# Two narrow projection slots: tokens stationary, or weights stationary and turned back

## The chip, the cores and the metric

The kernel runs on one core of a Trainium2 chip. The metric is the device time of one execution in microseconds (us). Five engines work side by side: TensorE (PE; its weight loads are listed apart as PEld), VectorE (DVE), ScalarE (ACT), GpSimd (POOL), and SyncE (SP), whose queue issues the DMAs here. Engines are ordered only by semaphores that the kernel sets and waits for by hand.

## The reference, cut to what matters

The network has 512 tokens of 1024 channels and eight sublayers: an even mixer, a SwiGLU, an odd mixer, a SwiGLU, an SSM mixer (Mamba-2), a SwiGLU, a convolution module and a SwiGLU. Each begins with a norm. Two places of it are touched.

In the even mixer one projection makes nine things from the normed tokens `h`:

```
aq, ak, av, bq, bk, bv, iq, ik, iw = split(h @ w_in, (512, 512, 512, 512, 64, 64, 512, 64, 8))
score = sum_h relu(iq_h @ ik.T * 64**-0.5) * (iw_h * 8**-0.5)      # picks the top 128 keys
yb    = softmax(bq_h @ bk.T ... over the picked keys) @ bv
```

`bv` (64 columns, the values) and `iw` (8 columns, the weights of the index heads) are needed with tokens on the partitions. In the SSM mixer the projection has 5152 columns, of which the last 32 are the time steps:

```
z, xbc, dt = split(h @ w_in, (2048, 3072, 32))
dt = softplus(dt + dt_bias)                 # (512 tokens, 32 heads)
a  = -exp(a_log);  y = scan(xs * dt, dt * a, bm, cm)
```

`dt`, too, is needed with tokens on the partitions. Everything is float32.

## The kernel before

**Layout.** `x_cm`, `h_hi` and `h_lo` hold activations channel-major: 8 chunks of 128 channels on the partitions, 512 tokens along the free axis. A normed activation is kept as two parts, `h_hi` (rounded to the float32r format) and `h_lo` (the rest).

**Slots.** Weights stream through two buffers in slots of up to 8 chunks of rows by 256 columns. For slot n SP loads `w_raw` (`load_slot`, L552 to L558; it waits until slot n-2 is split), ACT rounds it to `w_hi` in two halves (`round_half`, L1746 to L1758; it waits until slot n-2 is used), POOL subtracts to get `w_lo` in two halves (`low_part`, L804 to L810), and PE multiplies. `widths` names the two slots that are narrower than 256 columns: slot 1 with 72 and the first SSM slot with 32. ACT and POOL work on that width only. A product is three float32r matmuls per chunk: hi by hi, hi by lo, lo by hi.

**Two ways to multiply a slot.** `slot_cm` and `half_cm` keep 128 weight columns stationary and stream 512 tokens: 24 matmuls for 128 columns, and the result is channel-major. `slot_tok` (L1180 to L1194) keeps 128 tokens stationary and streams the weight columns: for each of 4 token tiles, 8 chunks, three matmuls, so 96 matmuls whatever the width, and the result is token-major, as `bv`, `iw` and `dt` want it.

```
for i in range(NT):
    for k in range(SLOT_K):
        pe.matmul(dst[i], h_hi[:, k, P*i:P*i+P], w_hi[parity][:, k, 0:width], ...)
        pe.matmul(dst[i], h_lo[:, k, P*i:P*i+P], w_hi[parity][:, k, 0:width], ...)
        pe.matmul(dst[i], h_hi[:, k, P*i:P*i+P], w_lo[parity][:, k, 0:width], ...)
```

**Even mixer.** `project` on PE (from L1272) runs slots 0 to 11 in order; slot 0 makes `bk` and `ik`, slot 1 `bv` and `iw`, slots 2 and 3 `iq`, slots 4 to 9 `bq`, `aq`, `ak`, slots 10 and 11 `av`. After each slot `after_even` sums one group of the conditioning projection (`ada_sums`, L1238), and after slot 2 `later_rows` turns parameter rows and waits for a scalar from DVE. ACT copies results out (`even_dest`, L1962), rounds the slot after next, and takes the roots for the head norms. DVE does the reciprocals of the head norms, a conditioning group of eight steps per slot (`ada_group`), and from slot 4 on adds index scores and takes the top keys (`index_add`, `take_top`).

**SSM mixer.** `ssm_pe` (L834) multiplies the dt slot first, each of its first 8 chunks as the norm on DVE delivers it (`h_chunk`, semaphore `h_ready`), into banks 0 and 1. Then come pieces d = 0 to 5 of a prologue (24 matmuls of 512 columns each, into bank d mod 3), with three small matmuls for the decays after d = 1 (L957), and then a scan of 18 steps in which further pieces fill gaps. DVE adds the bias to dt (L2070) when all 96 matmuls are done, and with ACT makes softplus and the log decay (L2073 to L2077). Piece 0 waits until DVE has read bank 0, and ACT rounds the slot of pieces 2 and 3 when the dt slot is used.

The order of work on every engine is fixed by the text of the program; no planner moves it.

Of the kernel before, what the change touches and what calls it, by code (L numbers as in the profile page):

```python
# [18 lines left out]
ALU = mybir.AluOpType  # L19
ACT = mybir.ActivationFunctionType  # L20
# [16 lines left out]
DI = 2048  # L37
MH = 32
# [87 lines left out]
def build(nc, t, out, sublayers=8):  # L126

    with ExitStack() as ctx:
        def sem(name):
            return ctx.enter_context(nc.semaphore(name))  # L130
# [206 lines left out]
        y_root = sem("y_root")  # L337
        sink_step = sem("sink_step")
        dt_step = sem("dt_step")
        dt_act = sem("dt_act")  # L340
        decay_sums = sem("decay_sums")
        decay_ready = sem("decay_ready")
# [149 lines left out]
        def ssm_loads(sp, load_slot):  # L492
            w = t["ssm_w_in_2"][0]
            n = SLOT["ssm"]
            load_slot(n, [(0, w[:, DI + 3072:DI + 3072 + MH])])
            for g in range(MG):
                at = n + 1 + 5 * g
                for j in range(2):
                    c0 = DI + S * g + SLOT_W * j
                    load_slot(at + j, [(0, w[:, c0:c0 + SLOT_W])])  # L500
                c0 = 2 * DI + P * g
                load_slot(at + 2, [(0, w[:, c0:c0 + P]), (P, w[:, c0 + S:c0 + S + P])])
                for j in range(2):
                    c0 = S * g + SLOT_W * j
                    load_slot(at + 3 + j, [(0, w[:, c0:c0 + SLOT_W])])
            for j, (m, k) in enumerate(OUT_ORDER):
                load_slot(SLOT["ssm_out"] + j, [(0, t["ssm_w_out_2"][0][1024 * k:1024 * k + 1024, 256 * m:256 * m + 256])])
# [3 lines left out]
        def _(sp):  # L511
# [60 lines left out]
            def load_swiglu(f):  # L572
# [31 lines left out]
                with sp.Fori(0, 2) as i:  # L604
# [8 lines left out]

            we = t["w_in_even"][0]
            even = [[(0, we[:, BK:BK + HD]), (64, we[:, BK:BK + HD]), (128, we[:, IK:IK + HD]), (192, we[:, IK:IK + HD])],
                    [(0, we[:, BV:BV + HD]), (64, we[:, IW:IW + I_HEADS])]]
            for c0 in (IQ, BQ, AQ, AK, AV):
                even += [[(0, we[:, c0 + 256 * j:c0 + 256 * j + 256])] for j in range(2)]
            for g in range(3):
# [50 lines left out]
        for g_ in range(MG):  # L670
            tok_slots |= {SLOT["ssm"] + 1 + 5 * g_ + 3, SLOT["ssm"] + 1 + 5 * g_ + 4}
            parts_of[SLOT["ssm"] + 1 + 5 * g_ + 2] = 2
        widths = {1: 72, SLOT["ssm"]: MH}
        loads_upto = {}
        count = [0, 0]
        for n in range(SLOT["end"]):
# [154 lines left out]
                        low_part(i * 6 + (n + j), (n + j) % 2, 8 if j % 3 < 2 else FC - 16, SLOT_W)  # L831
                n += N_DOWN

        def ssm_pe(pe, take, freed, slot_tok, slot_cm, h_chunk, follows):  # L834
            n0 = SLOT["ssm"]

            for m in range(2):
                take(m, dt_step, 1)
            dst = [bank[i // 2][:, SLOT_W * (i % 2):SLOT_W * (i % 2) + MH] for i in range(NT)]
            slot_tok(n0, dst, MH, h_chunk(4))  # L840

            def turn(d):

# [106 lines left out]
            for d in range(PROLOGUE):  # L950
                for f in range(8):
                    piece(d, f)
                if d == 1:
                    pe.wait_ge(dt_step, 3)
                    take(5, decay_ready, 1)
                    for j, tri in enumerate((upto, after, ones)):
                        ins = pe.matmul(bank[5][:, P * j:P * j + P], tri[:], log_decay[:].rearrange("p i h -> p (i h)"),  # L957
                                        start=True, stop=True)
                    ins.then_inc(decay_sums, 1)
# [176 lines left out]
        def _(pe):  # L1136
# [33 lines left out]
            def half_cm(n, m, dst):  # L1170
# [6 lines left out]
                    ins = pe.matmul(dst[:], lo, h_hi[:, k, :], start=False, stop=k == SLOT_K - 1)  # L1177
                ins.then_inc(w_used, 1)

            def slot_tok(n, dst, width, before=None):  # L1180

                parity = n % 2
                pe.wait_ge(w_split, 2 * n + 2)
                for i in range(NT):
                    for k in range(SLOT_K):
                        if before is not None and i == 0:
                            before(k)
                        a_hi_, a_lo_ = h_hi[:, k, P * i:P * i + P], h_lo[:, k, P * i:P * i + P]
                        b_hi_, b_lo_ = w_hi[parity][:, k, 0:width], w_lo[parity][:, k, 0:width]
                        pe.matmul(dst[i], a_hi_, b_hi_, start=k == 0, stop=False)  # L1190
                        pe.matmul(dst[i], a_lo_, b_hi_, start=False, stop=False)
                        ins = pe.matmul(dst[i], a_hi_, b_lo_, start=False, stop=k == SLOT_K - 1)
                    if i % 2 == 1:
                        ins.then_inc(w_used, 1)  # L1194
# [77 lines left out]
            def project(parts, nh, base_slot, qk_sq0, qk_root0, qk0, plain0, after_slot=None):  # L1272
# [12 lines left out]
                for s, part in enumerate(parts):  # L1285
                    n = base_slot + s
                    banks = (chunk % 4, (chunk + 1) % 4)
                    before = h_chunk(nh) if s == 0 else None
                    if part[0] == "tok":
                        width = part[1]  # L1290
                        per = 1 if width > P else 0
                        for m in range(2):
                            take(banks[m], plain_copied, plain0 + plain + 1 + m)
                        dst = [bank[banks[i // 2]][:, SLOT_W * (i % 2):SLOT_W * (i % 2) + width] for i in range(NT)]
                        slot_tok(n, dst, width, before)
                        plain += 2
                        while pending:
                            head_sums()
                    else:
                        dst = []  # L1300
                        for m in range(2):
                            if part[m] == "qk":
                                dst.append(take(banks[m], qk_normed, qk0 + qk + 1 + (m if part[0] == "qk" else 0)))
                            else:
                                plain += 1
                                dst.append(take(banks[m], plain_copied, plain0 + plain))
                        if before is not None:
                            slot_cm(n, n % 2, lambda k: h_hi[:, k, :], lambda k: h_lo[:, k, :], dst, before=before)
                        for m in range(2):
                            if before is None:  # L1310
                                half_cm(n, m, dst[m])
                            while pending:
                                head_sums()
                            if part[m] == "qk":
                                pending.append((qk_sq0 + qk, qk_root0 + qk))
                                qk += 1
                    chunk += 2
                    if after_slot is not None:
                        after_slot(s)
# [163 lines left out]
            def after_even(s):  # L1483
# [3 lines left out]
                if 4 <= s < 10:  # L1487
                    pe.wait_ge(plain_copied, 7)
                    for v in range(4 * (s - 4), 4 * (s - 4) + 4):
                        index_scores(v)  # L1490

            EVEN_PARTS = [("qk", "plain"), ("tok", 72), ("plain", "plain"), ("plain", "plain"), ("qk", "qk"), ("qk", "qk"),
                          ("qk", "qk"), ("qk", "qk"), ("qk", "qk"), ("qk", "qk"), ("tok", 256), ("tok", 256)]
            project(EVEN_PARTS, 0, 0, SQ_BASE["even"], ROOT_BASE["even"], 0, 0, after_even)

# [31 lines left out]
            if n_sub > 3:  # L1527
                swiglu(1, 3, follows(4))
            if n_sub > 4:
                ssm_pe(pe, take, freed, slot_tok, slot_cm, h_chunk, follows)  # L1530
            if n_sub > 5:
                swiglu(2, 5, follows(6))
            if n_sub > 6:
# [11 lines left out]
        def ssm_act(act, round_half):  # L1545
            n0 = SLOT["ssm"]
            act.wait_ge(bcast_in, 16 * 8)
            act.activation(alog_row[:], alog_row[:], ACT.Exp).then_inc(dt_act, 1)
            for m in range(2):
                round_half(n0 + 2, m)  # L1550

# [178 lines left out]
        def _(act):  # L1730
# [78 lines left out]
            def project(parts, base_slot, sq0, root0, qk0, dests, after_slot=None):  # L1809
# [12 lines left out]

                for s, part in enumerate(parts):
                    n = base_slot + s
                    if part[0] == "tok":
                        for m in range(2):
                            act.wait_ge(w_used, 2 * n + m + 1)
                            dests(s, m)
# [133 lines left out]
            def even_dest(s, m):  # L1962
                if s == 0:
                    act.activation(ik[:], bank[1][:], ACT.Copy).then_inc(plain_copied, 1)
                elif s == 1:
                    v = bank[2 + m][:].rearrange("p (i w) -> p i w", i=2)
                    act.activation(bv[:, 2 * m:2 * m + 2, :], v[:, :, 0:HD], ACT.Copy)
                    act.activation(iw[:, 2 * m:2 * m + 2, :], v[:, :, HD:HD + I_HEADS], ACT.Copy,
                                   scale=I_HEADS ** -0.5).then_inc(plain_copied, 1)
                elif s in (2, 3):  # L1970
                    c = 2 * (s - 2) + m
                    act.activation(iq[:, c, :], bank[(2 * s + m) % 4][:], ACT.Copy).then_inc(plain_copied, 1)
                else:
# [18 lines left out]
                    act.activation(neg_logit[v % 2][:, 0:w], bank[5 + v % 2][:, 0:w], ACT.Relu, scale=HD ** -0.5  # L1992
                                   ).then_inc(idx_relu, 1)

            EVEN = [("qk", "plain"), ("tok",), ("plain", "plain"), ("plain", "plain")] + [("qk", "qk")] * 6 + [("tok",), ("tok",)]
            project(EVEN, 0, SQ_BASE["even"], ROOT_BASE["even"], 0, even_dest, index_relu)
            act.wait_ge(w_used, 2 * N_EVEN)
            attention(2, 1, dict(s=0, t=0, y=0), A_HEADS, 0, lambda i: P * (i + 1), "diff", back=2)
# [64 lines left out]
        def ssm_dve(dve, link):  # L2063
            n0 = SLOT["ssm"]
            bc_tile = lambda row: row.unsqueeze(1).to_broadcast([P, NT, MH])

            dve.wait_ge(w_used, 2 * n0 + 2)
            for m in range(2):
                v = bank[m][:].rearrange("p (i w) -> p i w", i=2)[:, :, 0:MH]
                ins = dve.tensor_tensor(dt_tok[:, 2 * m:2 * m + 2, :], v, dtb_row[:].unsqueeze(1).to_broadcast([P, 2, MH]), ALU.add)  # L2070
            ins.then_inc(dt_step, 1)
            dve.wait_ge(dt_step, 1)
            dve.scalar_tensor_tensor(out=dt_abs[:], in0=dt_tok[:], scalar=-1.0, in1=dt_tok[:], op0=ALU.mult, op1=ALU.max  # L2073
                                     ).then_inc(dt_step, 1)
# [702 lines left out]
```

## Time and profile before

| | us |
|---|---|
| three runs | 3062.31, 3065.33, 3065.77 |
| median | 3065.33 |
| span of the profiled execution | 3062.3 |
| PE busy | 2800.6 (91% of the span) |
| DVE busy | 1417.1 (46%) |
| ACT busy | 1071.9 (35%) |
| POOL busy | 1077.0 (35%) |

The span runs from the first to the last instruction of the profiled execution; nothing else of that execution's own time is given beside it. The clock column of the profile is the share of full speed that was granted to TensorE: 1.00 is 2.4 GHz and 0.50 is 1.2 GHz. Start times of successive matmuls tell what each one costs in a dense stream, because their listed durations overlap.

### The profile page before, as it was taken

The page shows a single profiled execution, that of the slowest core. Times are in us where ns is not written, and L with a number is a line of the kernel's source. Part 1 is how long each engine was busy: PE and PEld are TensorE (multiplying, and loading weights), DVE is VectorE, ACT ScalarE, POOL GpSimd, SP SyncE. Part 2 cuts the span into 40 slices and gives each one's busy share as a digit, 9 for nine tenths or more (in the row PEclk, how much of TensorE's full clock was granted, in tenths as well). Part 3 has the DMA queues.
Part 4 walks back from the last instruction along what each step waited for, and adds up shares of the span by engine and source line. Part 5 has one row for each costly group of instructions (what it writes and reads, how often), then busy time and mean ns, then how long its engine had stood idle before and what let it go on. Part 6 is the DMA issues. An engine that isn't in the chain of part 4 may idle for free.

```text
span 3062.3 us, 34663 instructions
## 1 busy us (share of the span) xinstructions
PE 2800.6 (91%) x12655; PEld 2262.4 (74%) x12655; DVE 1417.1 (46%) x2167; ACT 1071.9 (35%) x1745; POOL 1077.0 (35%) x535
## 2 busy tenths in 40 slices
PE   4985689999999988999999999999999999799998
PEld 3764357777787667888878888888888765588886
DVE  6489872455412784222123566523331279533312
ACT  2221432322323474333223555523332322433321
POOL 1321000344443223444423565544444321144442
PEclk6897656999999999999988999999999999899998
DMA  7431040355433101223221221123322221122231
GB/s 215 138 110 55 1 138 14 97 164 164 137 100 85 63 28 56 83 82 110 94 74 55 69 69 56 56 83 100 105 91 92 86 63 41 42 96 96 96 97 55
DMA packets 277694, 264.50 MB, mean 86 GB/s; under 512 B 23020, under 2 KB 276557, under 8 KB 277581
## 3 DMA queue, kind: packets, MB, share of 16 engines
q1 hardware_dynamic: 277581, 262.97, 27.0%
q8 instruction: 74, 1.21, 0.2%
q14 instruction: 39, 0.32, 0.0%
HBM read 260.85 MB, written 2.10 MB: 86 GB/s over the span
## 4 chain that ended last, share of the span: by engine, by line
PE 71%; DVE 14%; issue 7%; DMA 3%; ACT 2%; POOL 2%; SPq 1%; DVEq 0%; ACTq 0%; POOLq 0%
PE bank L1151 17%; PE bank L1153 16%; PE bank L1152 16%; DMA root<-in_ada_w_dram 2%; DVE ada_acc L2392 2%; POOL w_lo L809 2%; PE bank L1099 1%; PE bank L883 1%; PE bank L885 1%; PE bank L884 1%; DVE bank L2216 1%; PE bank L1509 1%; DVE root L2398 1%; PE bank L1440 1%; DVE score L2575 1%
## 5 line engine op out<-in xcount | busy, mean ns | idle before, releaser
L809 POOL TENSOR_TENSOR w_lo<-w_raw,w_hi 128x1024 fp32r<-128x1024 f32 (+1 forms) x364 | 865.6, 2387 | 1674.2 <-ACT w_hi L1758 1103.3
L1151 PE MATMUL bank<-h_hi,w_hi 128*128 128x512 f32 x1632 | 651.6, 399 | 25.8 <-DVE h_lo L2359 11.6
L1152 PE MATMUL bank<-h_lo,w_hi 128*128 128x512 f32 x1632 | 645.4, 395 | 0.0
L1153 PE MATMUL bank<-h_hi,w_lo 128*128 128x512 f32 x1632 | 644.6, 395 | 0.0
L1758 ACT ACTIVATE w_hi<-w_raw 128x1024 fp32r<-128x1024 f32 (+1 forms) x232 | 232.2, 1014 | 510.7 <-PE bank L1153 438.9
L1151 PEld LDWEIGHTS bank<-h_hi,w_hi 128*128 128x128 f32 x1632 | 312.7, 192 | 95.7 <-issue 25.0
L1152 PEld LDWEIGHTS bank<-h_lo,w_hi 128*128 128x128 f32 x1632 | 313.1, 192 | 66.3 <-issue 1.7
L1153 PEld LDWEIGHTS bank<-h_hi,w_lo 128*128 128x128 f32 x1632 | 312.3, 191 | 66.5
L1153 PE MATMUL bank<-a_hi,w_lo 128*128 128x512 f32 x704 | 274.2, 389 | 0.0
L1151 PE MATMUL bank<-a_hi,w_hi 128*128 128x512 f32 x704 | 274.2, 389 | 0.0
L1152 PE MATMUL bank<-a_lo,w_hi 128*128 128x512 f32 x704 | 274.2, 389 | 0.0
L1927 ACT ACTIVATE w_hi<-w_raw 128x1024 fp32r<-128x1024 f32 x176 | 182.8, 1052 | 158.4 <-PE bank L1153 157.2
L2454 DVE TENSOR_TENSOR tmp<-sq,bank 128x512 f32<-128x512 f32 x88 | 60.5, 688 | 381.9 <-PE bank L1153 375.9
L2458 DVE TENSOR_TENSOR a_lo<-tmp,a_hi 128x512 f32 x88 | 167.4, 1914 | 22.0 <-ACT a_hi L1942 21.4
L1152 PEld LDWEIGHTS bank<-a_lo,w_hi 128*128 128x128 f32 x704 | 132.2, 188 | 27.6
L1153 PEld LDWEIGHTS bank<-a_hi,w_lo 128*128 128x128 f32 x704 | 132.2, 188 | 27.3
L1151 PEld LDWEIGHTS bank<-a_hi,w_hi 128*128 128x128 f32 x704 | 132.2, 188 | 27.3
L691 POOL TENSOR_TENSOR w_lo<-w_raw,w_hi 128x1024 fp32r<-128x1024 f32 x38 | 91.0, 2399 | 152.9 <-ACT w_hi L1758 152.9
L2216 DVE SCALAR_TENSOR_TENSOR bank<-u_pad,cols,bank 128x512 f32<-128x512 f32 x148 | 111.9, 756 | 5.3
L2392 DVE SCALAR_TENSOR_TENSOR ada_acc<-ada_w,cond,ada_acc 128x256 f32<-128x256 f32 x210 | 108.1, 515 | 8.8
L1937 ACT ACTIVATE sq<-bank 128x512 f32<-128x512 f32 x44 | 26.3, 598 | 237.6 <-DVE tmp L2454 237.4
L2496 DVE TENSOR_TENSOR x_cm<-bank,x_cm 128x512 f32<-128x512 f32 x16 | 11.1, 692 | 197.6 <-PE bank L1153 197.6
(352 smaller groups left out, 4671.3 us busy)
## 6 DMA issues: line engine op xcount, KB each, us to landing
ada_w<-in_ada_w_dram SPq DMA_DIRECT2D x60, 512.0 KB, 6.1
w_raw<-in_ffn_gate_dram SPq DMA_DIRECT2D x22, 1024.0 KB, 5.2
w_raw<-in_ffn_up_dram SPq DMA_DIRECT2D x22, 1024.0 KB, 5.2
w_raw<-in_ffn_w_gate_dram SPq DMA_DIRECT2D x22, 1024.0 KB, 5.1
w_raw<-in_ffn_w_up_dram SPq DMA_DIRECT2D x22, 1024.0 KB, 5.1
root<-in_ada_w_dram SPq DMA_DIRECT2D x144, 128.0 KB, 2.4
w_raw<-in_ffn_down_dram SPq DMA_DIRECT2D x16, 1024.0 KB, 5.1
w_raw<-in_ssm_w_in_dram SPq DMA_DIRECT2D x16, 1024.0 KB, 5.2
```

The source lines that it names most:

```text
L691: pool.tensor_tensor(w_lo[n % 2][:, :, half], w_raw[n % 2][:, :, half], w_hi[n % 2][:, :, half].bitcast(F32), ALU.subtract).then_inc(w_spl ...
L809: pool.tensor_tensor(w_lo[parity][:, 0:nk, half], w_raw[parity][:, 0:nk, half], w_hi[parity][:, 0:nk, half].bitcast(F32), ALU.subtract).th ...
L883: pe.matmul(bank[b][:], hi, s_hi, start=f == 0, stop=False)
L1151: pe.matmul(dst[m][:], hi, src_hi(k0 + k), start=first and k == 0, stop=False)
L1152: pe.matmul(dst[m][:], hi, src_lo(k0 + k), start=False, stop=False)
L1153: ins = pe.matmul(dst[m][:], lo, src_hi(k0 + k), start=False, stop=last and k == nk - 1)
L1758: act.activation(w_hi[n % 2][:, 0:nk, half], w_raw[n % 2][:, 0:nk, half], ACT.Copy).then_inc(w_rounded, 1)
L1927: act.activation(w_hi[par][:, :, half], w_raw[par][:, :, half], ACT.Copy).then_inc(w_rounded, 1)
L2216: link(dve.scalar_tensor_tensor(out=acc[:] if k < TAPS - 1 else v, in0=u_pad[:, c, k:k + S], scalar=tap(k), in1=acc[:], op0=ALU.mult, op1= ...
L2392: dve.scalar_tensor_tensor(out=acc[:], in0=w, scalar=cond[:, k:k + 1], in1=acc[:], op0=ALU.mult, op1=ALU.add).then_inc(ada_dve, 1)
L2454: dve.tensor_tensor(tmp[q][:], sq[q][:], bank[2 + q][:], ALU.mult).then_inc(gated, 1)
L2458: dve.tensor_tensor(a_lo[:, bass.ds(i * 2 + q, 1), :], tmp[q][:].unsqueeze(1), hi, ALU.subtract).then_inc(a_ready, 1)
```

## The change

Both narrow slots are multiplied with weights stationary by a new helper `one_cm`: 24 matmuls that stream 512 tokens, for 128 weight columns. The loads take 128 columns (neighbouring ones fill them up), `widths` becomes 128 for both, ACT copies the channel-major result from PSUM to SBUF, PE turns it with four transposes of 128 by 128, and the former readers take their columns from the turned bank.

In the even mixer slot 1 goes to its bank 2, ACT copies that to `score[:, 0, :]`, and PE turns it into bank 3 after the first half of slot 2. ACT copies `bv` and `iw` from there before it copies `iq`. In the SSM mixer the dt slot goes to bank 7, ACT copies it to `root[0]`, and PE turns it into bank 6 after the third of the eight chunks of piece 0; DVE reads it there in one instruction in place of two. The decay matmuls move from after piece 1 to after piece 2.

```
+        dt_cm_in, dt_turned, bv_cm_in, bv_turned = four new semaphores
...
-            load_slot(n, [(0, w[:, DI + 3072:DI + 3072 + MH])])
+            load_slot(n, [(0, w[:, DI + 3072 + MH - P:DI + 3072 + MH])])
...
-                    [(0, we[:, BV:BV + HD]), (64, we[:, IW:IW + I_HEADS])]]
+                    [(0, we[:, BV:BV + P - I_HEADS]), (P - I_HEADS, we[:, IW:IW + I_HEADS])]]
...
-        widths = {1: 72, SLOT["ssm"]: MH}
+        widths = {1: P, SLOT["ssm"]: P}
...
-            for m in range(2):
-                take(m, dt_step, 1)
-            dst = [bank[i // 2][:, SLOT_W * (i % 2):SLOT_W * (i % 2) + MH] for i in range(NT)]
-            slot_tok(n0, dst, MH, h_chunk(4))
+            one_cm(n0, take(7, dt_cm_in, 1), h_chunk(4))
+
+            def turn_dt():
+                pe.wait_ge(dt_cm_in, 1)
+                take(6, dt_step, 1)
+                for i in range(NT):
+                    ins = pe.transpose(bank[6][:, P * i:P * i + P], root[0][:, P * i:P * i + P], ident[:])
+                ins.then_inc(dt_turned, 1)
...
+                    if d == 0 and f == 2:
+                        turn_dt()
-                if d == 1:
+                if d == 2:
                     pe.wait_ge(dt_step, 3)
...
+            def one_cm(n, dst, before=None):
+                pe.wait_ge(w_split, 2 * n + 2)
+                for k in range(SLOT_K):
+                    if before is not None:
+                        before(k)
+                    hi, lo = w_hi[n % 2][:, k, 0:P], w_lo[n % 2][:, k, 0:P]
+                    pe.matmul(dst[:], hi, h_hi[:, k, :], start=k == 0, stop=False)
+                    pe.matmul(dst[:], hi, h_lo[:, k, :], start=False, stop=False)
+                    ins = pe.matmul(dst[:], lo, h_hi[:, k, :], start=False, stop=k == SLOT_K - 1)
+                ins.then_inc(w_used, 2)
...
+                    if part[0] == "bv":
+                        one_cm(n, take(banks[0], bv_cm_in, 1))
+                        take(banks[1], plain_copied, plain0 + plain + 2)
...
+                            if s == 2 and m == 0:
+                                pe.wait_ge(bv_cm_in, 1)
+                                for i in range(NT):
+                                    ins = pe.transpose(bank[3][:, P * i:P * i + P], score[:, 0, P * i:P * i + P], ident[:])
+                                ins.then_inc(bv_turned, 1)
...
+            act.wait_ge(w_used, 2 * n0 + 2)
+            act.activation(root[0][:], bank[7][:], ACT.Copy).then_inc(dt_cm_in, 1)
...
-                    v = bank[2 + m][:].rearrange("p (i w) -> p i w", i=2)
-                    act.activation(bv[:, 2 * m:2 * m + 2, :], v[:, :, 0:HD], ACT.Copy)
...
+                    if m == 0:
+                        act.activation(score[:, 0, :], bank[2][:], ACT.Copy).then_inc(bv_cm_in, 1)
...
+                    if s == 2 and m == 0:
+                        act.wait_ge(bv_turned, 1)
+                        v = bank[3][:].rearrange("p (i w) -> p i w", i=NT)
+                        act.activation(bv[:], v[:, :, 0:HD], ACT.Copy).then_inc(plain_copied, 1)
+                        act.activation(iw[:], v[:, :, P - I_HEADS:P], ACT.Copy, scale=I_HEADS ** -0.5
+                                       ).then_inc(plain_copied, 1)
...
-            dve.wait_ge(w_used, 2 * n0 + 2)
-            for m in range(2):
...
+            dve.wait_ge(dt_turned, 1)
+            dve.tensor_tensor(dt_tok[:], bank[6][:].rearrange("p (i w) -> p i w", i=NT)[:, :, P - MH:P], bc_tile(dtb_row[:]),
+                              ALU.add).then_inc(dt_step, 1)
```

## Rows read from the trace of the kernel before

**Rows 1.** The page: chain that ended last, by engine; granted clock in 40 slices.
```profile
PE 71%; DVE 14%; issue 7%; DMA 3%; ACT 2%; POOL 2%; SPq 1%; DVEq 0%; ACTq 0%; POOLq 0%
...
PEclk6897656999999999999988999999999999899998
```
**Rows 2.** Form and start times of `slot_tok`'s first matmul, over the whole span.
```profile
L1190 PE MATMUL bank<-w_hi,h_hi x160: 278/284/685, 79.4 to 1617.3; 128*128 128x256 f32 x96, 128*128 128x72 f32 x32, 128*128 128x32 f32 x32
```
**Rows 3.** Timeline (start, duration, engine, line) of PE in slot 1.
```profile
79.36 0.60 PE L1190 MATMUL bank<-w_hi,h_hi 128*128 128x72 f32 x1
...
84.03 0.28 PE L1190 MATMUL bank<-w_hi,h_hi 128*128 128x72 f32 x1
...
84.72 0.41 PE L1192 MATMUL bank<-w_lo,h_hi 128*128 128x72 f32 x1
...
95.60 0.41 PE L1192 MATMUL bank<-w_lo,h_hi 128*128 128x72 f32 x1
```
**Rows 4.** Timeline of PE in slot 2 and behind it.
```profile
96.67 0.77 PE L1175 MATMUL bank<-h_hi,w_hi 128*128 128x512 f32 x1
...
109.47 0.39 PE L1176 MATMUL bank<-h_lo,w_hi 128*128 128x512 f32 x1
109.70 0.39 PE L1177 MATMUL bank<-h_hi,w_lo 128*128 128x512 f32 x1
109.93 0.50 PE L1238 MATMUL bank<-ones,ada_acc 128*128 128x1 f32 x4
...
114.32 0.38 PE L1270 MATMUL bank<-lam_val,ones 1*128 1x1 f32 x2 [3.41 <-DVE lam_val L2527]
```
**Rows 5.** Timeline of PE from the dt slot through piece 0.
```profile
1594.43 0.37 PE L1190 MATMUL bank<-w_hi,h_hi 128*128 128x32 f32 x1 [2.85 <-DVE h_lo L2362]
...
1618.54 0.79 PE L883 MATMUL bank<-h_hi,w_hi 128*128 128x512 f32 x1 [0.45 <-DVE dt_tok L2070]
...
1623.40 0.61 PE L885 MATMUL bank<-h_hi,w_lo 128*128 128x512 f32 x1
1623.83 0.42 PE L883 MATMUL bank<-h_hi,w_hi 128*128 128x512 f32 x1
...
1626.82 0.39 PE L884 MATMUL bank<-h_lo,w_hi 128*128 128x512 f32 x1
```
**Rows 6.** Busy time of each engine in a window of the dt slot, then clock, DMA.
```profile
1604.00:1618.20 14.20, 14.09 (x67) 13.98 (x66) 0.07 (x1) 0.01 (x1) 0.00 (x0) 0.50 0.00 1
```
**Rows 7.** Timeline of DVE: end of the SSM norm, then softplus.
```profile
1600.49 1.29 DVE L2362 TENSOR_TENSOR h_lo<-sq,h_hi 128x512 fp32r<-128x512 f32 x2
...
1622.05 2.13 DVE L2076 SCALAR_TENSOR_TENSOR dt_tok<-dt_tok,dt_abs 128x128 f32<-128x128 f32 x1 [3.23 <-ACT dt_abs L1555]
```
**Rows 8.** Timeline of PE: four transposes, and the end of the SSM prologue.
```profile
1644.10 0.60 PE L849 MATMUL bank<-ident,tmp 128*128 128x128 f32 x4
...
1660.65 2.69 PE L905 MATMUL bank<-upto,root 128*128 128x128 f32 x14 [4.14 <-POOL root L701]
```
**Rows 9.** Timeline of DVE in the even mixer: norm of `bk`, a conditioning group beside POOL.
```profile
85.06 0.75 DVE L2400 SCALAR_TENSOR_TENSOR bk<-bank,qk_gain,root 128x512 f32<-128x512 f32 x1
...
97.24 7.68 DVE L2392 SCALAR_TENSOR_TENSOR ada_acc<-ada_w,cond,ada_acc 128x256 f32<-128x256 f32 x7
```
**Rows 10.** Waits of DVE, 124 to 330 us (total, times, longest), and the longest one.
```profile
DVE root L2398 <- ACT root L1820: 27.5, 4, 22.4
...
142.41 3.35 DVE L2398 RECIPROCAL root<-root 128x512 f32<-128x512 f32 x1 [22.38 <-ACT root L1820]
```
**Rows 11.** Timeline of the start: ACT and POOL on slot 1, DVE.
```profile
25.74 0.76 ACT L1758 ACTIVATE w_hi<-w_raw 128x288 fp32r<-128x288 f32 x2
...
29.65 2.04 POOL L809 TENSOR_TENSOR w_lo<-w_raw,w_hi 128x288 fp32r<-128x288 f32 x2
...
27.57 2.67 DVE L2409 TENSOR_TENSOR tmp<-tmp,sq 128x512 f32<-128x512 f32 x1 [7.74 <-ACT sq L1765]
30.16 0.88 DVE L2389 TENSOR_SCALAR ada_acc<-ada_w,cond 128x256 f32<-128x256 f32 x1
```

More of the change, by code:

```diff
@@ L339, in build @@
         dt_step = sem("dt_step")
+        dt_cm_in = sem("dt_cm_in")
+        dt_turned = sem("dt_turned")
+        bv_cm_in = sem("bv_cm_in")
+        bv_turned = sem("bv_turned")
         dt_act = sem("dt_act")
@@ L832, in _, with ssm_pe @@
                 n += N_DOWN
-        def ssm_pe(pe, take, freed, slot_tok, slot_cm, h_chunk, follows):
+        def ssm_pe(pe, take, freed, one_cm, slot_cm, h_chunk, follows):
             n0 = SLOT["ssm"]
-            for m in range(2):
-                take(m, dt_step, 1)
-            dst = [bank[i // 2][:, SLOT_W * (i % 2):SLOT_W * (i % 2) + MH] for i in range(NT)]
-            slot_tok(n0, dst, MH, h_chunk(4))
+            one_cm(n0, take(7, dt_cm_in, 1), h_chunk(4))
[5 more added lines that the diff above has]
+                ins.then_inc(dt_turned, 1)
             def turn(d):
@@ L1288, in project @@
                     before = h_chunk(nh) if s == 0 else None
-                    if part[0] == "tok":
+                    if part[0] == "bv":
+                        one_cm(n, take(banks[0], bv_cm_in, 1))
+                        take(banks[1], plain_copied, plain0 + plain + 2)
+                        plain += 2
+                        while pending:
+                            head_sums()
+                    elif part[0] == "tok":
                         width = part[1]
@@ L1490, in after_even @@
                         index_scores(v)
-            EVEN_PARTS = [("qk", "plain"), ("tok", 72), ("plain", "plain"), ("plain", "plain"), ("qk", "qk"), ("qk", "qk"),
+            EVEN_PARTS = [("qk", "plain"), ("bv",), ("plain", "plain"), ("plain", "plain"), ("qk", "qk"), ("qk", "qk"),
                           ("qk", "qk"), ("qk", "qk"), ("qk", "qk"), ("qk", "qk"), ("tok", 256), ("tok", 256)]
@@ L1529, in _ @@
             if n_sub > 4:
-                ssm_pe(pe, take, freed, slot_tok, slot_cm, h_chunk, follows)
+                ssm_pe(pe, take, freed, one_cm, slot_cm, h_chunk, follows)
             if n_sub > 5:
@@ L1824, in project @@
                     n = base_slot + s
-                    if part[0] == "tok":
+                    if part[0] in ("tok", "bv"):
                         for m in range(2):
@@ L1965, in even_dest @@
                 elif s == 1:
-                    v = bank[2 + m][:].rearrange("p (i w) -> p i w", i=2)
-                    act.activation(bv[:, 2 * m:2 * m + 2, :], v[:, :, 0:HD], ACT.Copy)
-                    act.activation(iw[:, 2 * m:2 * m + 2, :], v[:, :, HD:HD + I_HEADS], ACT.Copy,
-                                   scale=I_HEADS ** -0.5).then_inc(plain_copied, 1)
+                    if m == 0:
+                        act.activation(score[:, 0, :], bank[2][:], ACT.Copy).then_inc(bv_cm_in, 1)
                 elif s in (2, 3):
+                    if s == 2 and m == 0:
[4 more added lines that the diff above has]
+                                       ).then_inc(plain_copied, 1)
                     c = 2 * (s - 2) + m
@@ L1993, in index_relu @@
                                    ).then_inc(idx_relu, 1)
-            EVEN = [("qk", "plain"), ("tok",), ("plain", "plain"), ("plain", "plain")] + [("qk", "qk")] * 6 + [("tok",), ("tok",)]
+            EVEN = [("qk", "plain"), ("bv",), ("plain", "plain"), ("plain", "plain")] + [("qk", "qk")] * 6 + [("tok",), ("tok",)]
             project(EVEN, 0, SQ_BASE["even"], ROOT_BASE["even"], 0, even_dest, index_relu)
@@ L2065, in ssm_dve @@
             bc_tile = lambda row: row.unsqueeze(1).to_broadcast([P, NT, MH])
-            dve.wait_ge(w_used, 2 * n0 + 2)
-            for m in range(2):
-                v = bank[m][:].rearrange("p (i w) -> p i w", i=2)[:, :, 0:MH]
-                ins = dve.tensor_tensor(dt_tok[:, 2 * m:2 * m + 2, :], v, dtb_row[:].unsqueeze(1).to_broadcast([P, 2, MH]), ALU.add)
-            ins.then_inc(dt_step, 1)
+            dve.wait_ge(dt_turned, 1)
+            dve.tensor_tensor(dt_tok[:], bank[6][:].rearrange("p (i w) -> p i w", i=NT)[:, :, P - MH:P], bc_tile(dtb_row[:]),
+                              ALU.add).then_inc(dt_step, 1)
             dve.wait_ge(dt_step, 1)
```

## The prediction

> **What bounds the kernel now.** I read the page first. The chain that ended last is 71% PE and 14% DVE, and PE is granted full speed in most slices; the weakest ones lie in the first quarter, around the even mixer, and in a dip near the middle, where the SSM mixer begins [rows 1]. So time taken from PE counts wherever DVE or a load isn't late instead. Then I read the two slots in the order of their instructions. `slot_tok` streams 72 columns in one and 32 in the other, 32 times for its first matmul, so 96 matmuls each [rows 2].
>
> Slot 1 starts at 79.36 at full speed. The 38 matmuls after its second (about 79.79) take 0.11 us each up to 84.03. From 84.72 on the engine is at the lower level although it hasn't paused: the last 51 take (95.60 - 84.72) / 51 = 0.213 us each [rows 3]. So the price is not the columns but the load of 128 columns of weights before each matmul, and it doubles when the clock goes from 2.4 to 1.2 GHz. The dt slot never gets out of the lower level: 14 us of unbroken PE work at a grant of 0.50 [rows 6], from 1594.43 to the first piece at 1618.54 [rows 5]. Dense 512-column matmuls take 0.227 us at the higher level [rows 4] and 0.43 at the lower (1618.54 to 1623.40 in 11 steps, the first of them 0.59) [rows 5].
>
> DVE: up to 142.41 it waits for PE's and ACT's results, once for 22.4 us, and of the waits from 124 to 330 us only 5.1 us are left behind that one: from there DVE sets the even mixer's pace [rows 10].
>
> **Even mixer, slots 1 and 2.** `one_cm` is 24 matmuls: 79.36 + 0.43 + 23 x 0.227 = 85.0. The conditioning sums between slots take 0.36 at the higher level (109.93 to the next work at 110.29), so PE asks for bank 0 at 85.4. That bank is free when DVE has normed `bk`, at 85.06 + 0.75 = 85.8 [rows 9], a wait that nobody saw before because slot 2 started at 96.67 [rows 4]. Slot 2 then runs its 48 matmuls without the slow start that it had: 85.9 + 48 x 0.227 = 96.8; before it took 13.3 us. Four transposes between its halves cost 0.45 (the same four of a piece are listed with 0.60, the end of the last included) [rows 8]. They wait for ACT's copy of the bank, which starts near 85.1 and takes some 0.6, so it lies under slot 2's first half. Sum: slot 2 ends at 97.2 in place of 109.9 [rows 4], 12.7 us earlier.
>
> What else moves: ACT rounds slot 3 some 11 us earlier, so POOL's part of it now lies beside the conditioning group that DVE runs from 85.8. That pairing is what stretched the next group to 7.68 us before [rows 9]; it changes place, it isn't added. ACT makes two copies (bv, iw) behind the transposes and only then rounds slot 4, about 1 us later than it could, with PE on slot 2's second half and slot 3 for over 15 us. The 3.41 us in which PE waits for DVE's scalar behind slot 2 hang on ACT's work after slot 2 and stay [rows 4]. From slot 4 on DVE is the pace, but its first job there waited 22.4 us for PE and ACT [rows 10]; 12.7 of these can go and 9.7 remain to cover a conditioning group that slips by its 4 us beside POOL. So the shift passes into the DVE chain: +12.7 gained; bounds 0 (all of it met by DVE) and 13.2.
>
> **Start.** Slot 1 is loaded and split before the first norm, where DVE has one chain up to 58 us. ACT rounds 2 x 288 elements per partition in 0.76 and then squares x; DVE starts at 27.57 when these arrive, and its first two instructions are long (2.67 and 0.88 us) while POOL runs until 31.7 [rows 11]. 288 elements become 512: on ACT some 0.2 more each, on POOL 2.04 / 2 = 1.02 becomes 1.3 to 1.5, so 0.6 to 1.0 more in all. I take 0.8 lost; bounds 0 (DVE slips through) and 1.5 (both in series, and the larger load landing late).
>
> **SSM mixer, dt slot and piece 0.** The norm on DVE ends at 1600.49 + 1.29 = 1601.8 [rows 7]. `one_cm` takes three matmuls per chunk, 1.28 us at the lower level, about the pace at which chunks come (the last two come closer together), so it is a dense 512-column stream from 1594.43 on. In piece 0 the same kind of stream was granted full speed after 5.3 us, by 1623.83 [rows 5]; here that would be near 1600. Then the last chunks follow the norm: 1601.8 + 3 x 0.227, with some lag of the rise, 1602.9. Piece 0 no longer waits for DVE: it begins at 1602.9 and takes 24 x 0.227 = 5.4 plus four transposes 0.45 [rows 8]: 1608.8. Before it ended at 1626.82 + 0.23 = 1627.0 [rows 5]. Gain 18.2 us, of which 15.6 are the slot and 3.1 the slow start of piece 0, less 0.45.
>
> Off the path: ACT's copy (0.6) lies under the first three chunks of piece 0 (2.0), whose cover is thin only if ACT is late. Softplus was stretched to 2.13 us beside POOL [rows 7] and will be so again; it ends near 1610, 1.2 after piece 0, so DVE's convolution of piece 0 starts late by that, with two pieces (10.9 us) before bank 0 is asked for again. The decay matmuls after piece 2 cost PE what they cost after piece 1. The dt slot is rounded and split at full width while PE still has 8 us of SwiGLU work. At the end of the prologue PE waits 4.14 us for POOL [rows 8], whose last job was started by ACT's rounding after PE's last piece; that wait moves along with the pieces. Nothing afterwards hangs on a fixed time. Bounds: 12.9 (no full speed before piece 0 begins: slot ends at 1604.7, piece 0 costs 8.5 + 0.9) and 18.6.
>
> [...]
>
> **Sum.** 12.7 - 0.8 + 18.2 = 30.1 us. Against the profiled execution's span 3062.3 that is 3032.2; the median stands 3.0 above the span, so 3035.2.
>
> **Rivals.**
> Cold restart: the chunk-paced slot isn't dense enough, or the copy and transposes break the stream, and piece 0 runs slow as before. For it: PE fell to the lower level in slot 1 without a pause [rows 3]. Against: the new stream has 512 columns in each matmul. Gain 12.7 - 0.8 + 12.9 = 24.8: 3040.5.
> DVE takes the even gain: two stretched conditioning groups and the scalar chain end later than PE needs, and slot 4's roots find DVE busy. For: DVE sets the pace after 142 us. Against: 22.4 us of waiting just before [rows 10]. Gain 18.2 - 0.8: 3047.9.
> No change: beside that, the SSM prologue is held by POOL and ACT splitting its slots rather than by PE. Against: PE has no such wait in the prologue before its end [rows 8]. About 3065.
> Slower: the clock. The thin streams around the new waits (0.4 us for bank 0, the copy, the transposes) leave PE at 1.2 GHz behind both places. Each 512-column matmul then costs 0.2 us more than in my sum, so it decides from 150 matmuls on. Pieces 0 to 5 and slots 2 and 3 are 240: 3035.2 + 48 = 3083. For: the level was lost under work once. Against: every dense 512-column stream in these rows got out of it.
>
> **How the numbers follow.** Forecast 0.66, cold restart 0.17, DVE 0.11, no change 0.03, slower 0.03. A measurement of this kernel can tell about 0.2%, 6 us, from no change; the first three cases are faster by more: 0.94, 0.03, 0.03. The best sum is 13.2 + 18.6 = 31.8 and the runs of before lie up to 3 below their median, so the low end is 3029.5; the high end takes in the cold restart and part of the DVE case: 3044.
>
> **What would show it.** Right: slot 1's 24 matmuls end near 85 and slot 2's near 97; a wait of about 0.4 us on the norm of `bk`; the 22.4 us wait of DVE shrinks to about 10; the first norm starts less than 1 us late; the dt slot ends near 1591 on the new clock (1602.9 less 11.9) with piece 0 at 0.227 us per matmul from its start; later stages keep their lengths. Wrong: pieces at 0.43 us, a PE wait on ACT's copy above 0.5 us, DVE's chain without its wait, or a stage far behind that grows.

## The result and the profile after

The changed kernel takes 3033.05 us (median of 4 runs, 3027.76 to 3038.96) beside 3064.34 of the kernel before (4 runs, 3062.31 to 3065.77). The ratio is 0.9896, 95% interval 0.9881 to 0.9911: 31.9 us less, with an interval of 27.3 to 36.5. Forecast were 30.1 us less and 3035.2, between 3029.5 and 3044. The profiled execution is the shortest of the four, 3027.76 us with a span of 3025.8.

The page, with the two lines that answer to [rows 1]:

```profile
PEclk6996757999999998999999999999999999899999
...
PE 72%; DVE 15%; issue 5%; ACT 2%; DMA 2%; POOL 1%; SPq 1%; DVEq 0%; ACTq 0%; POOLq 0%
```

The shape is the same; the two slices at 8 in the middle of the span, at the dt slot, are gone. Next, PE in the even mixer (start, duration, engine, line, operation; L1197 to L1199 are `one_cm`, L1343 the transposes). These rows answer to [rows 3, 4]:

```profile
78.53 0.79 PE L1197 MATMUL bank<-h_hi,w_hi 128*128 128x512 f32 x1
...
84.20 0.39 PE L1199 MATMUL bank<-h_hi,w_lo 128*128 128x512 f32 x1
84.43 0.50 PE L1260 MATMUL bank<-ones,ada_acc 128*128 128x1 f32 x4
85.04 0.50 PE L1185 MATMUL bank<-h_hi,w_hi 128*128 128x512 f32 x1
...
90.63 0.60 PE L1343 MATMUL bank<-ident,score 128*128 128x128 f32 x4
...
96.90 0.62 PE L1288 MATMUL bank<-ident,rows 128*128 128x128 f32 x4
102.28 0.58 PE L1292 MATMUL bank<-lam_val,ones 1*128 1x1 f32 x2 [4.76 <-DVE lam_val L2564]
```

Slot 1 lasts 84.43 - 78.53 = 5.9 us in place of 16.5, and slot 2 starts 0.25 us after the sums at its own pace. The wait for the scalar has grown from 3.41 to 4.76. DVE beside it, first two rows of the kernel before (its first group, and the scalar), then the changed kernel, answering to [rows 9] and [rows 10]:

```profile
86.10 3.68 DVE L2392 SCALAR_TENSOR_TENSOR ada_acc<-ada_w,cond,ada_acc 128x256 f32<-128x256 f32 x7
...
113.21 0.88 DVE L2526 TENSOR_TENSOR lam_val<-lam_exp 1x1 f32<-1x1 f32 x1 [7.79 <-ACT lam_exp L1983]
```

```profile
85.28 7.75 DVE L2429 SCALAR_TENSOR_TENSOR ada_acc<-ada_w,cond,ada_acc 128x256 f32<-128x256 f32 x7
...
93.33 7.81 DVE L2429 SCALAR_TENSOR_TENSOR ada_acc<-ada_w,cond,ada_acc 128x256 f32<-128x256 f32 x7
...
101.91 0.15 DVE L2563 TENSOR_TENSOR lam_val<-lam_exp 1x1 f32<-1x1 f32 x1 [0.27 <-ACT lam_exp L2022]
...
130.53 3.35 DVE L2435 RECIPROCAL root<-root 128x512 f32<-128x512 f32 x1 [22.32 <-ACT root L1855]
```

Both conditioning groups are now stretched, where one was; the scalar comes behind them, and no longer waits for ACT (0.27 us in place of 7.79). DVE's first root of slot 4 is at 130.53 in place of 142.41: 11.9 us earlier.

In the SSM mixer (answering to [rows 5]; the transposes are L847, the pieces L891 to L893):

```profile
1575.12 0.77 PE L1197 MATMUL bank<-h_hi,w_hi 128*128 128x512 f32 x1 [2.85 <-DVE h_lo L2399]
...
1580.38 0.54 PE L1197 MATMUL bank<-h_hi,w_hi 128*128 128x512 f32 x1
...
1583.50 0.39 PE L891 MATMUL bank<-h_hi,w_hi 128*128 128x512 f32 x1
...
1585.55 0.60 PE L847 MATMUL bank<-ident,root 128*128 128x128 f32 x4
1585.90 0.47 PE L891 MATMUL bank<-h_hi,w_hi 128*128 128x512 f32 x1
```

The dt slot lasts 8.4 us in place of 24.1 to the first piece, the clock rises inside it, and piece 0 ends at 1589.4, 14.3 us after the slot's start; before it was 32.6. ACT's copy is never waited for.

The stages in between, by the windows of both profiles from one norm's reciprocal to the next (length, then busy time of PE, PEld, DVE, ACT, POOL, then clock, DMA share and GB/s). Before:

```profile
59.53:561.63 502.10, 400.96 (x1624) 303.74 (x1624) 333.99 (x645) 155.88 (x324) 74.36 (x32) 0.73 0.25 80
561.63:967.99 406.36, 386.48 (x1680) 319.35 (x1680) 173.22 (x223) 116.11 (x142) 165.47 (x68) 0.96 0.43 132
967.99:1217.05 249.06, 220.25 (x1056) 171.88 (x1056) 158.16 (x317) 131.65 (x336) 68.23 (x56) 0.92 0.14 47
1217.05:1589.27 372.22, 367.14 (x1608) 304.06 (x1608) 90.62 (x76) 115.29 (x142) 158.53 (x69) 0.98 0.28 91
1589.27:2422.76 833.49, 808.11 (x4178) 687.71 (x4178) 332.65 (x464) 337.20 (x476) 386.32 (x202) 0.97 0.25 79
```

After:

```profile
59.96:545.75 485.79, 382.93 (x1556) 286.93 (x1556) 336.58 (x645) 156.13 (x323) 74.51 (x32) 0.75 0.26 82
545.75:955.15 409.40, 387.88 (x1680) 320.11 (x1680) 172.09 (x223) 116.33 (x142) 165.87 (x68) 0.95 0.43 131
955.15:1200.21 245.06, 215.98 (x1056) 167.96 (x1056) 158.51 (x318) 131.40 (x336) 67.85 (x55) 0.94 0.15 48
1200.21:1570.07 369.86, 364.79 (x1608) 301.99 (x1608) 90.65 (x76) 115.96 (x142) 159.54 (x69) 0.99 0.29 92
1570.07:2386.30 816.23, 793.49 (x4110) 671.99 (x4110) 331.44 (x462) 338.62 (x477) 387.73 (x203) 0.98 0.26 80
```

The first stage loses 16.3 us and the fifth 17.3. The three between hold no edited instruction, yet they read +3.0, -4.0 and -2.4, with the same work and a slightly different clock. In the ten profiles of this study these three stages together last from 1024.3 to 1034.6 us (both kernels here near the low end: 1027.6 and 1024.3), by no order that fits the edits. So of the 36.5 us between the two profiled spans 3.3 lie in stages that weren't edited; the medians differ by 31.3. The first stage holds such a piece too: 3.3 of its 16.3 us come from a stretch without an edited instruction, behind the root of slot 4, where this execution was granted the higher clock and the kernel before was not (shown with `e6_lam_later` below).

### The profile page after: what moved, and what is told of

It is laid out like the page before. It is cut to its first block, busy times and chain, and to the rows that moved or that the text cites. A ratio compares the mean times of both kernels' runs of the same rounds, so it can differ in the third digit from the quotient of the medians.

```text
span 3025.8 us, 34391 instructions
## 1 busy us (share of the span) xinstructions
PE 2761.3 (91%) x12519; PEld 2222.9 (73%) x12519; DVE 1417.1 (47%) x2166; ACT 1074.5 (36%) x1745; POOL 1080.6 (36%) x535
## 4 chain that ended last, share of the span: by engine, by line
PE 72%; DVE 15%; issue 5%; ACT 2%; DMA 2%; POOL 1%; SPq 1%; DVEq 0%; ACTq 0%; POOLq 0%
PE bank L1161 18%; PE bank L1162 17%; PE bank L1163 17%; DVE ada_acc L2429 2%; DMA root<-in_ada_w_dram 2%; DVE root L2435 1%; PE bank L1109 1%; PE bank L891 1%; DVE bank L2253 1%; PE bank L893 1%; PE bank L892 1%; PE bank L1542 1%; POOL w_lo L813 1%; PE bank L1473 1%; DVE score L2612 1%
## 5 line engine op out<-in xcount | busy, mean ns | idle before, releaser
L2533 DVE TENSOR_TENSOR x_cm<-bank,x_cm 128x512 f32<-128x512 f32 x16 | 11.1, 692 | 197.6 <-PE bank L1163 197.6
```

## The experiments

Each was run beside the kernel before on one chip. Ratios are to the kernel before.

**Each part alone.** `e1_even_only` is the changed kernel with the dt slot put back; `e2_ssm_only` has slot 1 put back.

```
e1:  -            one_cm(n0, take(7, dt_cm_in, 1), h_chunk(4))
     +            slot_tok(n0, dst, MH, h_chunk(4))          # and its load, width, reader, no copy by ACT, decays after d = 1
e2:  -            EVEN_PARTS = [("qk", "plain"), ("bv",), ...
     +            EVEN_PARTS = [("qk", "plain"), ("tok", 72), ...   # and its load, width, copies
```

> The even mixer's part alone; the SSM mixer as before. Theory A (both parts pay at their own place and add up): the gain is 12.7 of PE less 0.8 at the start = 11.9 us, ratio 0.9961, DVE's first root of slot 4 near 130.5 in place of 142.4. Rival B (one place took nearly all, the rest is drift of the clock between the stages): here either under 6 or over 20 us. Rival C (the parts need each other, because a stage in between runs differently): this and the SSM part alone add up to clearly less than the 31.3 us between the medians.

> The SSM mixer's part alone; the even mixer as before. Theory A: 18.2 us, ratio 0.9941; the dt slot lasts about 8.4 us on PE, piece 0 runs at 0.227 us per matmul, and the scan's first segments start 18 us earlier counted from the dt slot's start. Rival B: under 10 or over 25 us. Rival C: with the even part alone clearly less than 31.3 us in sum.

Measured: the even part alone 0.9958 (0.9943 to 0.9973), 12.9 us; the SSM part alone 0.9943 (0.9927 to 0.9959), 17.5 us. Their sum is 30.4 us, and each lies within 1 us of its term, though each interval is some 5 us wide to either side. DVE's first root of slot 4 comes at 132.35 with the even part and at 142.61 without it: 10.1 us earlier than in the kernel before, where 11.9 were expected. The scan's first segments start 48.3 us after the dt slot, 17.9 us sooner than before. From the norm before the SSM mixer to the next one listed it is 833.76 us with the old dt slot and 816.48 with the new. So the parts pay where they stand, and rival B is out. That they add up (rival C) agrees with the medians, 30.4 against 31.3, whose intervals alone could hide some us; in the profiles the SSM stage shrinks by 17.0 us alone and by 17.3 with the other part, and the root moves by 10.1 alone and by 11.9.

**The price of a narrow slot: columns, weight loads or clock.** `e3_tok128` and `e4_tok256` are the kernel before with wider narrow slots, tokens still stationary.

```
-        widths = {1: 72, SLOT["ssm"]: MH}
+        widths = {1: W, SLOT["ssm"]: W}       # W = 128 or 256, with loads and readers to match
```

> The kernel before, tokens stationary, but both narrow slots stream 128 columns in place of 72 and 32 (the same wider loads, rounding and splitting as in the changed kernel, no other edit). Theory A (a matmul with weights of its own costs the weight load, 0.11 us at 2.4 GHz and 0.213 at 1.2, whatever its columns): both slots cost the same or less; if 128 streamed columns keep the clock up they take 96 x 0.11 = 10.6 us, so up to 5.7 us less for slot 1 and up to 10 less for the dt slot, ratio 0.995; if not, ratio 1.000. Rival D (the columns are the price): 128 columns take 1.8 and 4 times the time of 72 and 32: slower by over 10 us.

> The same with 256 streamed columns in both slots, the width of every other token-stationary slot. Theory A: 256 columns take as long as a weight load at either clock (0.11 at 2.4 GHz, 0.213 at 1.2), so the slots cost 96 x 0.11 = 10.6 us if the clock stays up, which I expect here: slot 1 about 10.7 us in place of 16.3, the dt slot about 14 in place of 23.5; less 2 us for full-width rounding and splitting at the start: gain about 12 us, ratio 0.996. Rival E (the clock falls for another reason than few streamed columns, as the many weight loads): both slots stay at 0.213 us per matmul and the kernel is 0 to 3 us slower than before.

Measured: 128 columns 0.9978 (0.9959 to 0.9996), 256 columns 0.9955 (0.9939 to 0.9971). Streaming 1.8 to 8 times the columns made the kernel faster. In slot 1 the clock is the whole difference. The windows have the same columns as above; first the kernel before, in slot 1, then 128 columns:

```profile
79.40:84.40 5.00, 5.00 (x45) 4.76 (x43) 2.73 (x1) 2.24 (x4) 4.68 (x2) 1.00 0.00 0
84.80:95.80 11.00, 11.00 (x53) 11.00 (x53) 4.62 (x10) 0.35 (x2) 0.00 (x0) 0.50 0.62 192
```

```profile
79.30:84.30 5.00, 5.00 (x45) 4.76 (x43) 2.74 (x1) 2.23 (x4) 4.70 (x2) 1.00 0.00 0
84.30:90.30 6.00, 6.00 (x56) 6.00 (x56) 5.02 (x10) 0.35 (x2) 0.00 (x0) 1.00 0.84 265
...
1596.00:1606.00 10.00, 10.00 (x49) 10.00 (x48) 0.00 (x0) 0.00 (x0) 0.00 (x0) 0.50 0.00 0
```

At full speed 72 and 128 columns take the same (45 matmuls in 5 us), so the streamed columns are not the price; what is left is the load of 128 weight columns before each matmul. That it is the load itself, and not another fixed cost of the pair, is argued: no run has a narrow stream with fewer weight columns. With 72 the engine, busy all the time, is put back to 1.2 GHz and does 53 in 11 us; with 128 it stays up and slot 1 is 5.4 us shorter (next work at 90.32 against 95.82, from starts at 79.25 and 79.36). But in the dt slot, which begins at the lower level, the same 128 columns never bring it up (last row): 24.2 us from start to first piece, as before. With 256 columns slot 1 runs at full speed too (first row below, 0.12 us per matmul and not 0.11), and in the dt slot the clock comes up 9.8 us in:

```profile
83.00:94.00 11.00, 11.00 (x94) 11.00 (x94) 7.76 (x10) 1.95 (x5) 4.44 (x2) 1.00 0.52 162
...
1593.00:1602.50 9.50, 8.30 (x31) 6.83 (x32) 7.26 (x12) 4.67 (x7) 0.00 (x0) 0.50 0.41 108
1602.70:1611.40 8.70, 8.25 (x67) 8.05 (x67) 0.65 (x3) 0.63 (x1) 0.00 (x0) 1.00 0.01 2
```

That slot takes 18.2 us to the first piece, not the 14 that I expected, because it is slow for half of it; and at the start the full width costs 3.0 us (first norm at 62.57 in place of 59.53), not 2. So rivals D and E are out. Of theory A's two cases for 128 columns, clock kept and clock not kept, each slot showed one; with 256 columns the clock was expected to stay up, and in the dt slot it had yet to rise. It also prices the alternative: simply widening the two slots is worth 13.8 us (0.0045 of 3063.7), under half of the change (interval 8.9 to 18.7).

**The changed kernel again, and three versions beside it.**

> The changed kernel again, beside the next three on one chip. Both readings of the first result expect 0.988 to 0.991 of before: 30.1 us by the sum of the two places (0.9902), 31.9 by the first interval.

Measured: 0.9905 (0.9885 to 0.9924), 29 us (23 to 35). Both readings fit.

`e5_narrow`: only the needed weight columns are loaded, rounded and stationary.

```
-                    hi, lo = w_hi[n % 2][:, k, 0:P], w_lo[n % 2][:, k, 0:P]
-                    pe.matmul(dst[:], hi, h_hi[:, k, :], ...)
+                    hi, lo = w_hi[n % 2][:, k, 0:cw], w_lo[n % 2][:, k, 0:cw]      # cw = 72 and 32
+                    pe.matmul(dst[0:cw, :], hi, h_hi[:, k, :], ...)
```

> The changed kernel with the old loads and widths: 72 and 32 weight columns stationary, results on 72 and 32 partitions, turned from there. Theory: a matmul of 512 streamed columns costs the same whatever the number of its weight columns, so the slots keep their 0.227 us per matmul; the start gets back what the wider slot 1 cost it, so the first norm's reciprocal comes at 59.5 in place of 60.0 us and the four transposes take no more than 0.45. Against the changed kernel 0.5 to 1 us faster. Rival: fewer columns or rows in use let the clock fall, then slot 2 or piece 0 starts at 0.43 us per matmul and it is 2 to 6 us slower.

Measured: 0.9900 (0.9885 to 0.9915), which alone doesn't tell it from the changed kernel; the profile does. The first norm's reciprocal comes at 59.34 in place of 60.06 in the changed kernel run again, the four transposes (72 wide) take 0.42 in place of 0.60, and the slots keep their pace: piece 0 starts at full speed, so the rival is out. The start, first the changed kernel run again, then this one:

```profile
28.11 1.72 DVE L2446 TENSOR_TENSOR tmp<-tmp,sq 128x512 f32<-128x512 f32 x1 [8.31 <-ACT sq L1800]
29.75 1.36 DVE L2426 TENSOR_SCALAR ada_acc<-ada_w,cond 128x256 f32<-128x256 f32 x1
31.15 4.56 DVE L2429 SCALAR_TENSOR_TENSOR ada_acc<-ada_w,cond,ada_acc 128x256 f32<-128x256 f32 x7
35.62 0.68 DVE L2446 TENSOR_TENSOR tmp<-tmp,sq 128x512 f32<-128x512 f32 x1
```

```profile
27.38 2.67 DVE L2446 TENSOR_TENSOR tmp<-tmp,sq 128x512 f32<-128x512 f32 x1 [7.67 <-ACT sq L1800]
29.97 0.88 DVE L2426 TENSOR_SCALAR ada_acc<-ada_w,cond 128x256 f32<-128x256 f32 x1
30.89 4.09 DVE L2429 SCALAR_TENSOR_TENSOR ada_acc<-ada_w,cond,ada_acc 128x256 f32<-128x256 f32 x7
34.89 0.68 DVE L2446 TENSOR_TENSOR tmp<-tmp,sq 128x512 f32<-128x512 f32 x1
```

DVE's squares arrive 0.73 us later with the wide slot, but all of that is taken up by the first instruction, which was long beside POOL anyway (1.72 in place of 2.67): the next one starts at 29.75, even 0.22 sooner. What POOL's wider work adds comes back in the next two lines (1.36 for 0.88, and 4.56 for 4.09). At the end of the stretch it is 35.62 against 34.89: 0.7 us, the term for the start.

`e6_lam_later`: PE takes DVE's scalar after slot 3.

```
                 if s == 2:
                     later_rows()                # without its wait for the scalar
+                if s == 3:
+                    lam_spread()                # the wait and the matmul
```

> The changed kernel with PE's wait for DVE's scalar moved from behind slot 2 to behind slot 3; only the parameter rows are still turned after slot 2. Theory: the wait was 4.76 us in the changed kernel (3.41 before), lengthened because both conditioning groups now run beside POOL; it goes, and slot 3 no longer starts at the lower clock, 1.5 to 2 us. Gain 6 to 7 us over the changed kernel, DVE's first root of slot 4 near 124. Rival: DVE, which now waits for PE's matmul before its next conditioning group, is late for slot 4 and takes part of it back: under 3 us.

Measured: 0.9866 (0.9849 to 0.9883), 0.9961 of the changed kernel by the ratio of the two, about 11 us where I expected 6 to 7. The root of slot 4 came at 123.81 in place of 131.19, 7.4 us earlier. Of these 0.5 were there when slot 1 began (78.54 and 79.03), so the edit's part is 6.9, as the theory has it; before the scalar's matmul PE has no wait left:

```profile
108.26 0.50 PE L1260 MATMUL bank<-ones,ada_acc 128*128 128x1 f32 x4
108.69 0.38 PE L1295 MATMUL bank<-lam_val,ones 1*128 1x1 f32 x2
```

The rival, that DVE takes it back, is out: DVE still waited 7.18 us before that root. The other 4 us aren't shown to be the edit's. The two intervals leave room for them, and 3.2 of them can be seen in the profiles: from that root to DVE's first logits of the attention (the row below, with its start) it takes either 169.5 us or 172.4 to 172.9, and the changed kernel has both. First the profile with the result, then the changed kernel run again, then this version:

```profile
300.05 0.29 DVE L2671 SCALAR_TENSOR_TENSOR neg_logit<-dist,bank 128x128 f32<-128x128 f32 x1
```

```profile
303.87 0.29 DVE L2671 SCALAR_TENSOR_TENSOR neg_logit<-dist,bank 128x128 f32<-128x128 f32 x1
```

```profile
293.25 0.29 DVE L2676 SCALAR_TENSOR_TENSOR neg_logit<-dist,bank 128x128 f32<-128x128 f32 x1
```

Less their roots (130.53, 131.19 and 123.81) that is 169.5, 172.7 and 169.4. The other seven profiles, the kernel before among them (315.27 - 142.41 = 172.9), have 172.4 to 172.9. Against the first profile of the changed kernel the edit gives 6.8 us here, against the second 10.6.

What decides between the two lengths is the granted clock right behind that root. The first 4 us of the stretch, the profile with the result and then the changed kernel run again:

```profile
130.53:134.53 4.00, 3.71 (x16) 2.93 (x17) 3.96 (x2) 0.51 (x2) 0.38 (x1) 1.00 0.64 182
```

```profile
131.19:135.19 4.00, 3.71 (x9) 2.59 (x10) 3.96 (x2) 0.52 (x2) 0.38 (x1) 0.50 0.62 180
```

PE is busy equally long, but does 16 matmuls in one and 9 in the other, and in the second the grant is back at 1.00 only some 6.5 us behind the root. Behind it the third root of the stretch waits 2.20 us for ACT in the second and not at all in the first. Of the ten profiles the two with the short length, the first here and `e6_lam_later`, were granted 1.00 in these 4 us, and the eight others 0.50 to 0.57 (the kernel before 0.51). In the 5 us ahead of the root PE was busy for 3.2 in each of them, so why the grant fell in one execution and held in the other stays open. It is no effect of the edits: the same kernel shows both.

`e8_all`: both edits, and ACT squares before it rounds slot 1.

```
-            round_slots(-2, 2)
-            norm_squares(0)
+            round_slots(-2, 1)
+            norm_squares(0, 0, 3)
+            round_slots(-1, 1)
+            norm_squares(0, 3, DC)
```

> The narrow form and the later scalar together, and at the start ACT rounds slot 1 only after the first three squares of x. Theory: 0.5 to 1 us plus 6 to 7 us plus at the start about 1 us, because DVE's first addition comes some 1.2 us sooner; the first norm's reciprocal near 58.5 to 59.0. About 8 us under the changed kernel, 0.987 of before. Rival: POOL's four splits hold DVE up just as long wherever they lie, so nothing is gained at the start.

Measured: 0.9866 (0.9847 to 0.9884), 3024.92 us beside 3064.7, the same as `e6_lam_later` (3024.37) as far as these runs tell. The start:

```profile
26.84 1.03 DVE L2453 TENSOR_TENSOR tmp<-tmp,sq 128x512 f32<-128x512 f32 x1 [7.29 <-ACT sq L1805]
27.79 2.44 DVE L2433 TENSOR_SCALAR ada_acc<-ada_w,cond 128x256 f32<-128x256 f32 x1
...
34.68 0.69 DVE L2453 TENSOR_TENSOR tmp<-tmp,sq 128x512 f32<-128x512 f32 x1
```

The first addition is 0.5 us sooner than with the narrow slot alone and short (1.03), and the next instruction is long in its place (2.44 for 0.88): 34.68 against 34.89, 0.2 us, where about 1 was expected. POOL's second piece of slot 0 runs from 27.28 to 30.07 there, and the long instruction of DVE ends at 30.23, right behind it. So the rival holds for the order, and of the first norm's way from 60.06 to 59.12 the narrow slot has 0.72. The Trainium skill says in "SBUF — State Buffer", section "Who interferes with whom", that VectorE and GpSimd share a pair of ports, and that whichever instruction has it keeps it to its end while the other blocks. The trace agrees: moving the instruction moved the wait, from 2.67 and 0.88 us to 1.03 and 2.44.

## Why the prediction was right, by its steps

- Slot 1 at 0.227 us per matmul: right. 5.9 us with its first one, against 5.6 forecast. Its start was 0.8 us earlier, though the first norm came 0.4 later: slot 0, which the change doesn't touch, took 1.3 us less (18.6 from the norm to slot 1, 19.8 before; in the ten profiles 18.6 to 19.8).
- Bank 0, which was to hold PE back by 0.4 us: PE begins 0.25 us after the sums' slot, at 85.04, when DVE has normed `bk` (84.23 + 0.75 = 84.98). Right place, and 0.25 for 0.4.
- Slot 2 without its slow start, transposes at 0.45: 96.54 with them, 11.5 us; forecast 11.35.
- Nothing of the scalar wait moves: wrong. Forecast 3.41, measured 4.76 and 4.75, because I let the two groups beside POOL only change places, and hung the wait on ACT. Both groups are stretched now (7.75 and 7.81), and the scalar hangs on them and not on ACT. It cost 1.35 us, which no other term gave back. That the sum for the root still came out at 11.9 is luck: slot 1 had begun 0.8 us earlier. With the changed kernel run again it was 11.2, with the even part alone 10.1. Counted from the start of slot 1 the root moved by 11.1, 10.9 and 10.5 us in the three, against 12.7 in the sum.
- Start, 0.8 us: measured 0.43 in the first profile, 0.53 in the second, 0.7 against the narrow form.
- DVE doesn't take the shift: right. Its wait before slot 4 was expected to shrink from 22.4 to about 10, and it did not (22.32). That sign was wrong though the conclusion held: DVE's earlier jobs hang on PE as well, the last group among them, and moved along. Nor does DVE alone set the pace from there on, as I read it: a clock that held for TensorE behind that root was worth 3.3 us.
- dt slot: end at 8.4 us after its start, forecast 8.5; clock rise 5.3 us in, forecast 5.3 to 6 (in two of the other profiles already near 3, with the slot no shorter, since its last chunks follow the norm); piece 0 in 5.9 us with the transposes. From the slot's start to the end of piece 0 18.3 us less, forecast 18.2. By the next norm 17.3 are left; of the missing 1.0, 0.4 is gone by the scan's first segments, and the rest is not located. The wait at the end of the prologue moved along as forecast (4.13 and 4.14). The slot itself ended at 1583.5 and not near 1591: what ran before it had gained 7.4 us more than the 11.9 at the root, 3.3 by the clock behind the root and 3.3 in the three stages without an edit, so the sign that later stages keep their lengths did not hold.
- Rivals: cold restart didn't happen in any profile; the even gain was not taken by DVE; the run with 128 columns shows that the mechanism of the slower case, a level lost and not regained under work, exists; it came with narrow streams (128 columns, 24 us at 0.50), and no 512-column stream of this change stayed at the lower level.
- Range: the best sum, 31.8, and 3 us below the median of before give 3065.3 - 31.8 - 3 = 3030.5, not the 3029.5 of the forecast. The result lies above either.

Both terms had the right mechanism. The SSM term had the right size; the even term, counted from slot 1, is 1.6 to 2.2 us smaller than its sum, by the scalar wait above all. The located gains, 10.1 to 11.9 up to the root and 17 to 18.4 in the SSM stage, add up to 27 to 30 us; that the first median shows 31.9 is within its interval, and its profiled execution had 3.3 us more by the clock.

## What to carry to other kernels

When the free side of a product is narrower than the stationary side, price it by its weight loads, and put the long side into the stream: 24 matmuls of 512 columns and four transposes took 6.3 us in slot 1 and 8.8 in the dt slot, where 96 narrow ones took 16 and 24. Look at the granted clock over each stretch of narrow matmuls: in slot 1 half the loss (5.4 of 10.6 us) was that TensorE ran at 1.2 GHz while busy. When a stage is pulled forward, ask which scalar or small result it will now outrun, and move the consumer back one slot; that was worth 7 us at its place here.

## What the runs showed of the hardware that I had not expected

- 128 streamed columns per weight load kept the full clock through the 11 us of slot 1, where it had been granted, and the dt slot, which began at the lower level, stayed there for its 24 us. With 256 columns the dt slot was at full speed from 9.8 us on (its first 7 us had gaps, waiting for the norm), with 512 from 3 to 6 us on in the six profiles that have it. These are stretches of this kernel, with its other work around them, and no limit is read from them.
- One and the same kernel had the clock held at 1.00 behind the root of slot 4 in one execution and lowered to 0.50 in another, with equal work ahead of it; it moved everything behind by 3.2 us.
- Stages with no edited instruction differ by up to 10 us in sum between profiles of nearly the same program (1024.3 to 1034.6), so a single profiled span can mislead by a third of this gain. The shift of the root of slot 4 repeated to 1.8 us counted from the start of the span, and to 0.5 counted from the start of slot 1.
